# A two-block network on one core: four plain feed-forward tiles instead of three, a shorter wait at product boundaries, and the probability copies of the mixers moved to one engine

## The reference, cut to what matters

```
# first block (16 meta tokens ahead of the 1024)
h  = h + rmsnorm(z @ w_out, mix_norm_post)
u  = rmsnorm(h, ffn_norm_pre)                     # 1024 features
gt = causal_dwconv(u @ w_gate, conv_w, conv_b)    # 3 taps, 2816 features
y  = (gelu(gt) * (u @ w_up)) @ w_down
h  = h + rmsnorm(y, ffn_norm_post)
# second block, per block of 128 tokens
att: logits = q k^T/8 - slope*dist (previous and own block of keys), softmax with a sink,
     out = p @ v                                  # 8 heads of 64
mlstm: chunks, decays exp(b_t - b_s + i_s), state c_new = decay*c + (k*w)^T v
x = x + concat(rms(att), sigmoid(o)*rms(mlstm)) @ w_out
x = x + cross_attention(x, mem);  x = x + top-2 mixture of 32 experts
```

## Time and profile before

| what | value |
|---|---|
| median of 3 runs | 2849.12 us (2843.03 to 2854.50) |
| the profiled execution | 2844.58 us, its span 2842.8 us |
| PE busy in the span | 2667.1 us (94%) |
| DVE busy | 1919.3 us (68%) |
| ACT busy | 1284.8 us (45%) |
| POOL busy | 711.7 us (25%) |
| mean granted clock of TensorE | 0.974 |

### The profile page before, as it was taken

How to read it: one execution, slowest core, us unless ns; L and a number is a source line. 1 busy time by engine, 2 the same in 40 slices (tenths; PEclk the granted TensorE clock), 3 DMA queues, 4 the chain that set the end, 5 groups by cost and what they waited for, 6 DMA issues and landing times. The chain is left out here.

```text
span 2842.8 us, 38460 instructions
## 1 busy us (share of the span) xinstructions
PE 2667.1 (94%) x14346; PEld 2310.5 (81%) x14346; DVE 1919.3 (68%) x2417; ACT 1284.8 (45%) x1968; POOL 711.7 (25%) x446
## 2 busy tenths in 40 slices
PE   8989999999879999999989998889998999999993
PEld 7989999899768888878868887767785688888882
DVE  5366556363388777777884723766355899999996
ACT  4242332332343233234544204764332577777773
POOL 3000000002255555513620000005400244444441
PEclk9999999999989999999999999999998999999997
DMA  5342323343212222266742111114203799999996
GB/s 186 108 133 90 100 97 101 119 138 119 96 45 75 81 89 76 80 216 198 232 140 67 45 60 67 39 45 141 74 18 141 272 422 417 416 415 415 413 413 242
DMA packets 267201, 472.04 MB, mean 166 GB/s; under 512 B 24338, under 2 KB 183330, under 8 KB 241970
## 3 DMA queue, kind: packets, MB, share of 16 engines
q1 hardware_dynamic: 257554, 435.49, 42.8%
q0 software_dynamic: 9504, 34.61, 3.0%
HBM read 398.61 MB, written 71.43 MB: 165 GB/s over the span
## 5 line engine op out<-in xcount | busy, mean ns | idle before, releaser
L4084 DVE TENSOR_TENSOR k_w_lo<-k_raw,k_w_hi 128x2048 fp32r<-128x2048 f32 x192 | 433.4, 2287 | 34.6 <-ACT k_w_hi L4020 31.0
L4020 ACT CAST k_w_hi<-k_raw 128x2048 fp32r<-128x2048 f32 x192 | 363.2, 1912 | 64.3 <-PE bank L3938 41.3
L120 PE MATMUL bank<-u_hi,p_w_hi 128*128 128x342 f32 (+2 forms) x720 | 236.9, 329 | 8.9 <-DVEq L889 6.0
L121 PE MATMUL bank<-u_lo,p_w_hi 128*128 128x342 f32 (+2 forms) x720 | 231.1, 321 | 0.0
L122 PE MATMUL bank<-u_hi,p_w_lo 128*128 128x342 f32 (+2 forms) x720 | 230.8, 321 | 0.0
L3936 PE MATMUL bank<-k_w_hi,k_x_hi 128*128 128x512 f32 x512 | 203.0, 397 | 1.3 <-DVE k_x_lo L4090 1.0
L3938 PE MATMUL bank<-k_w_hi,k_x_lo 128*128 128x512 f32 x512 | 199.8, 390 | 0.0
L3937 PE MATMUL bank<-k_w_lo,k_x_hi 128*128 128x512 f32 x512 | 199.3, 389 | 0.0
L1467 PE MATMUL bank<-u_ffn_hi,f_w_hi 128*128 128x512 f32 (+3 forms) x520 | 170.7, 328 | 16.8 <-DVE f_inner L1757 8.4
L1468 PE MATMUL bank<-u_ffn_lo,f_w_hi 128*128 128x512 f32 (+3 forms) x520 | 167.2, 322 | 0.0
L1469 PE MATMUL bank<-u_ffn_hi,f_w_lo 128*128 128x512 f32 (+3 forms) x520 | 166.7, 321 | 0.0
(11 more groups left out here) (620 smaller groups left out, 7502.7 us busy)
## 6 DMA issues: line engine op xcount, KB each, us to landing
k_raw<-in_w_e_gate_dram SPq DMA_DIRECT2D x64, 1024.0 KB, 7.1
k_raw<-in_w_e_up_dram SPq DMA_DIRECT2D x64, 1024.0 KB, 7.7
k_raw<-in_w_e_down_dram SPq DMA_DIRECT2D x64, 1024.0 KB, 8.3
f_raw<-in_ffn_w_down_dram SPq DMA_DIRECT2D x77, 256.0 KB, 3.0
p_w<-in_w_in_dram SPq DMA_DIRECT2D x34, 512.0 KB, 4.4
f_raw<-inner_scratch SPq DMA_DIRECT2D x55, 256.0 KB, 3.5
f_raw<-in_ffn_w_gate_dram SPq DMA_DIRECT2D x22, 512.0 KB, 3.7
f_raw<-in_ffn_w_up_dram SPq DMA_DIRECT2D x22, 512.0 KB, 4.9
```

Source lines behind the costliest of these rows:

```text
L120: pe.matmul(out, wh[:, t, :], xh[t][:, c:c + n], start=t == 0, stop=False)
L121: pe.matmul(out, wh[:, t, :], xl[t][:, c:c + n], start=False, stop=False)
L4020: act.copy(wh[:, q, :], raw[:, r, :]).then_inc(hi_made, 1)
L4084: dve.tensor_tensor(wl[:, q, :], raw[:, r, :], wh[:, q, :], ALU.subtract).then_inc(lo_made, 1)
```

## The change

Three parts of the program are edited.

*Feed-forward.* Tile 3 joins `PLAIN` (`FAST_FROM = 4`), with banks of its own in `GATE` and `UP`. Tile 1 reads the same unscaled slices as tile 0; VectorE multiplies its gate by `token` in the new `keep_gate(1)` and its inner value in `multiply(1)`. So `stream_high(k)` waits until tile 1 has used slice k (`u_used` >= 8 + k + 1), and the streamed slices are first read by tile 2's gate, whose first third waits for them one by one. All `stream_low` and `sums_low` are VectorE's; GpSimd has only the low parts of weights. TensorE's wait for the first four low parts stands behind the first sum of squares, and VectorE's `low(0)` before `scale(1)`. The order of VectorE and ScalarE between tile 0 and the first tile of `seven` is new.

*Down.* TensorE no longer waits at the end of a product; ScalarE waits for `mm` or `used`, whichever belongs to the step (`multiplied`).

*Mixers.* `turn` comes in two pairs: groups 0 and 1 right after `write(i)`, groups 2 and 3 after `scores(i+1, (2, 3))` and `att_sums`. VectorE makes all four copies, two after `update(i)` and two after `logits(i+1, (2, 3))`; `keep_odd` is gone. `keys` and `h_back` use T[1], `weigh` T[0]. At the start ScalarE does `decays(0)` and `keys(0)` ahead of the exponentials, VectorE `front(0)` ahead of the second logits, and the memory's transposes are spread through iteration 0.

```diff
-PLAIN = (0, 1, 2, KF - 1)
+PLAIN = (0, 1, 2, 3, KF - 1)
+FAST_FROM = 4
@@ stage_ffn
+    GATE = {0: (0, 1, 2), 1: (5, 6, 7), 2: (2, 3, 4), 3: (0, 1, 7), KF - 1: (0, 1, 3)}
+    UP = {0: (3, 4), 1: (0, 1), 2: (5, 6), 3: (5, 6), KF - 1: (4, 5)}
@@ gpsimd
-            for q in (4, 5, 6, 7):
-                low(q)
-            for k in range(2, KD):
-                stream_low(k)
-            low(8)
-            low(9)
-            sums_low(0)
-            low(10)
-            low(11)
-            sums_low(2)
-            for q in range(12, first_operand(KF - 1) + 4):
+            for q in range(4, first_operand(KF - 1) + 4):
                 low(q)
@@ tensor
+                if n == 1 and k == 0:
+                    pe.wait_ge(g_kept, 1)            # in row_tile, before the up part
+                    if n == 2 and e == 0 and j == 1:
+                        pe.wait_ge(inner_made, 1)    # in column_tile
+                        if n == 2 and e == 0 and j == 0:
+                            pe.wait_ge(v_lo, k + 1)
-            pe.wait_ge(lo_made, 4)
             pe.wait_ge(logs, NL)
             pe.sem_inc(sq_used, 2)
...
+                if k == 0:
+                    pe.wait_ge(lo_made, 4)
                 pe.wait_ge(u_lo, k + 1)
                 row_tile(0, k)
...
+            pe.wait_ge(lo_made, 14)
+            pe.wait_ge(inner_made, 2)
+            column_tile(3, 0, LIVES, GATE[3], 0).then_inc(gmm, 1)
+            pe.wait_ge(lo_made, 16)
+            pe.wait_ge(inner_made, 3)
+            column_tile(3, 1, SEQS, UP[3], TAPS - 1).then_inc(umm, 1)
@@ scalar
-                act.wait_ge(u_used, k + 1)
+                act.wait_ge(u_used, KD + k + 1)
@@ scalar, the order after the table load
+            high(6), high(7), stream_high(0..2), gelu(0), stream_high(3), high(8), high(9), stream_high(4..7), high(10), high(11)
+            sums_high(0), gelu(1), keep_gate(2), sums_high(1), high(12), high(13), gelu(2), high(14), high(15)
+            sums_high(2), sums_high(3), keep_gate(3), high(16..19)
@@ vector, the order after the factor
+            keep_gate(0), stream(0..3), conv(0), stream(4), stream(5), stream_low(0), stream(6), stream_low(1), stream(7)
+            stream_low(2..4), multiply(0), stream_low(5..7), keep_gate(1), conv(1), sums(0), sums(1), multiply(1)
+            sums_low(0), sums_low(1), conv(2), sums(2), multiply(2), sums(3), sums_low(2), sums_low(3)
+            combine(4, 0..3), conv(3)
@@ Down, stage_down
+    def multiplied(self, engine, step):
+        i, j = divmod(step, HALF_K)
+        if j == HALF_K - 1:
+            engine.wait_ge(self.mm, 4 * (i + 1))
+        else:
+            engine.wait_ge(self.used, (HALF_K - 1) * i + j + 1)
-                else:
-                    pe.wait_ge(mm, 4 * (i + 1))
-                    pe.sem_inc(d.used, 1)
@@ stage_mixers, tensor
-                    pe.wait_ge(pt_kept_odd, 2 * c)
+                    pe.wait_ge(pt_kept, 4 * c - 1)   # keys
                 write(i)
+                turn(i, (0, 1))
                 if i < LAST:
                     scores(i + 1, (2, 3))
                 if i:
                     att_sums(i - 1)
-                turn(i)
+                else:
+                    memory_turn(0)
+                turn(i, (2, 3))
@@ stage_mixers, vector
                 update(i)
+                keep(i, (0, 1))
                 if i < LAST:
                     logits(i + 1, (2, 3))
-                keep(i)
+                keep(i, (2, 3))
@@ stage_mixers, scalar
+            decays(0)
+            keys(0)
             exponentials(0, 0)
             exponentials(0, 1)
-            decays(0)
-            keys(0)
-                keep_odd(i)
```

More of the change, by code:

```diff
@@ L1402, in std @@
         def std(n):
[L1403 removed]
+            return PLAIN.index(n) - 1
         @block.sync
@@ L1646, in _ @@
             act.preload_act_table(ACT.Gelu_apprx_tanh)
-            stream_high(0)
-            stream_high(1)
             high(6)
             high(7)
-            for k in range(2, KD):
+            for k in range(3):
                 stream_high(k)
+            gelu(0)
+            stream_high(3)
             high(8)
             high(9)
-            gelu(0)
-            sums_high(0)
-            keep_gate(1)
+            for k in range(4, KD):
+                stream_high(k)
             high(10)
             high(11)
+            sums_high(0)
+            gelu(1)
+            keep_gate(2)
             sums_high(1)
-            gelu(1)
+            high(12)
+            high(13)
+            gelu(2)
+            high(14)
+            high(15)
             sums_high(2)
             sums_high(3)
-            keep_gate(2)
-            for q in range(12, 16):
+            keep_gate(3)
+            for q in range(16, 20):
                 high(q)
@@ L1803, in fast, with keep_gate @@
                 conv(n)
+            def keep_gate(n):
+                dve.wait_ge(gmm, n + 1)
+                if n:
+                    dve.wait_ge(conv3, n)
+                for j, (c, w) in enumerate(LIVES):
+                    x = dve.tensor_tensor(g[:, c:c + w], bank[GATE[n][j]][:, 0:w], token[:, c:c + w], ALU.mult)
+                x.then_inc(g_kept, 1)
             dve.wait_ge(rstd_made, NL)
@@ L1818, in _ @@
             dve.wait_ge(h_made, KD)
-            stream(0)
-            stream_low(0)
-            dve.wait_ge(gmm, 1)
-            for j, (c, w) in enumerate(LIVES):
-                m = dve.tensor_tensor(g[:, c:c + w], bank[GATE[0][j]][:, 0:w], token[:, c:c + w], ALU.mult)
-            m.then_inc(g_kept, 1)
-            stream(1)
-            stream_low(1)
-            for k in range(2, KD):
-                stream(k)
-            dve.wait_ge(g_kept, 1)
-            conv(0)
+            keep_gate(0)
+            for k in range(4):
+                stream(k)
+            conv(0)
+            stream(4)
+            stream(5)
+            stream_low(0)
+            stream(6)
+            stream_low(1)
+            stream(7)
+            for k in range(2, 5):
+                stream_low(k)
+            multiply(0)
+            for k in range(5, KD):
+                stream_low(k)
+            keep_gate(1)
+            conv(1)
             sums(0)
-            multiply(0)
             sums(1)
-            conv(1)
+            multiply(1)
+            sums_low(0)
             sums_low(1)
+            conv(2)
             sums(2)
-            multiply(1)
+            multiply(2)
             sums(3)
+            sums_low(2)
             sums_low(3)
             for j in range(4):
-                combine(3, j)
-            conv(2)
+                combine(FAST_FROM, j)
+            conv(3)
             for n in FAST:
@@ L2716, in write, with turn @@
                 m.then_inc(umm, 1)
-            def turn(n):
-                for g in range(4):
-                    if g == 0 and n:
-                        pe.wait_ge(scaled, n)
-                    if g == 1:
+            def turn(n, groups):
+                for g in groups:
+                    if g == 0:
                         if n:
@@ L2891, in update, with keep @@
                 m.then_inc(state, 1)
-            def keep(n):
-                for g in (0, 2):
+            def keep(n, groups):
+                for g in groups:
                     dve.wait_ge(turned, 4 * n + g + 1)
@@ L2920, in _ @@
             logits(0, (0, 1))
+            front(0)
+            logits(0, (2, 3))
             maxima(0, 0)
-            logits(0, (2, 3))
-            maxima(0, 1)
-            front(0)
             queries(0)
             weights(0)
+            maxima(0, 1)
             for i in range(NB):
```

165 lines of the change are left out of this document (69 added, 96 removed).

## The result

The changed kernel takes 2828.26 us (median of 6 runs, 2825.37 to 2836.11) against 2849.84 us of the kernel before in the same session (6 runs, 2843.03 to 2855.86). The ratio is 0.9931, with a 95% interval from 0.9913 to 0.9950: faster, by 21.6 us by the medians and 19.7 us by the ratio (14.3 to 24.8). Forecast were 2828 us. The profiled execution took 2828.68 us, its span is 2826.8 us.

What follows compares the result with a forecast made beforehand. VectorE's list was taken to bound the way in, TensorE the steady tiles and nearly stage_down, a VectorE and ScalarE chain the mixers. Way in -15.0, stage_down -3.2, mixers -2.7: -20.9 from 2849.12 gives 2828 us; range 2819 to 2842.

Steps and rivals of the forecast that it cites:

- The start, -2.2: Way in: ScalarE's first square no longer waits behind four low parts of weights; 2.2 us sooner, at most 2.5.
- Tile 2's wait for the streamed slices: Way in: TensorE waits some 4.5 us in tile 2's first third for VectorE's low slices, GpSimd costing VectorE 5.9 us.
- Tile 3 as a plain tile hides VectorE's list: Way in: plain tile 3 hides its waits by a few us; tile 4 starts 15.0 us sooner.
- stage_down, -3.2: stage_down: gaps at six product boundaries go, 0.46 to 0.65 us each, 3.2 us in all; bounds 0 and 3.9.
- Mixers, +0.35 an iteration: Mixers at full clock: two copies of 0.60 us join VectorE's chain, idle of 0.75 and 0.1 goes; four iterations +1.4.
- Mixers, late iterations, -2.4: Mixers: two iterations of 20.09 us at low clock get 1.2 us shorter each, since transposes and `weigh` start sooner.
- Mixers, the start, -1.7: Mixers' start: first read 3.3 us sooner, second read 1.7 us sooner as iteration 0 is bound by ScalarE.
- Mixers, last iteration, 0: Mixers' last iteration: VectorE's copies end when they did before, so no change.
- (a): Rival, way in: VectorE keeps up, tile 2 has no wait, 7.3 us more gained, 2821 us; chance 0.13.
- (b): Rival, way in: VectorE later than counted, blocked for whole instructions or late for tile 3; gain 10 or less, 2833 to 2836; chance 0.17.
- (c): Rival, mixers: they give nothing back, 0.35 us in each of six iterations, no gain at start, +2, 2833 us; chance 0.11.
- (d): Rival, mixers: VectorE's longer chain lowers TensorE's clock, some 9 us more an iteration, six give 2882 us; chance 0.04.

Runs made afterwards that it cites:

- vector_lows: The changed kernel with the six low parts of weights q 6 to 11 on VectorE instead of GpSimd; 2825.47 us, one run.
- three_plain: The changed kernel with three plain tiles ahead of those of seven products instead of four, tile 3 being one of seven again; 2838.15 us, one run.
- last_group_scalar: The changed kernel with the copy of the fourth group of probabilities on ScalarE, the other three on VectorE; 2824.29 us, one run.
- old_start: The changed kernel with the old order at the mixers' start, exponentials ahead of decays and keys, front after both halves of the logits; 2829.82 us, one run.
- best: The changed kernel with low parts q 6 to 11 on VectorE and, from iteration 1 on, the fourth group's copy on ScalarE; 2820.16 us, 4 runs.
- both_better: The changed kernel with low parts q 6 to 11 on VectorE and the fourth group's copy on ScalarE in iteration 0 too; 2821.99 us, one run.

## Why the prediction was right, step by step

- *The start, -2.2:* right; the first square sum came 2.56 sooner, and slice 1 then waited 0.36 for VectorE's low part, the very operation named.
- *Tile 1 without a gap, -13.4:* right, no gap ahead of it nor of tile 2, and its end 13.2 us sooner after the project's sums.
- *Tile 2's wait for the streamed slices:* right in place, releaser and size: 5.2 us lost to GpSimd against 5.9, a gap of 4.16 us against some 4.5. vector_lows shows the cause: with six lows off GpSimd the loss is gone. The mechanism was wrong, and the size came near by luck. I had VectorE go on at 0.42 of its pace for the 2.02 us of each low part; the trace shows the two engines taking turns, VectorE's operation ending 1.08 to 1.09 us after GpSimd's. The 2.02 us of the earlier trace rows hold GpSimd's own wait for VectorE (alone it takes 1.29), so a low part holds one operation of VectorE up by 1.0 to 1.1 us, five times here: 5.2. My 5.9 also isn't my own count: five and a half low parts at 1.2 are 6.4 to 6.6. The Trainium skill (SBUF — State Buffer, "Who interferes with whom") has the two exclude each other for whole instructions, and the trace agrees. What did not come is the -10 that I took from it: it priced each low part at its recorded 2.02 us, with GpSimd's own waiting in it.
- *Tile 3 as a plain tile hides VectorE's list:* right; three_plain shows what it costs without it. The sum of the way in was -15.0, measured -15.1 in the first pair of traces; over all of them tile 4 stands at 123.85 to 124.87 us with this part and 139.93 to 140.45 without, a gain of 15.1 to 16.6.
- *stage_down, -3.2:* right in sum, -3.1, by two errors that cancel. A boundary is worth 0.64, not 0.53 on the mean. (The 0.46 at the lower end left out the 0.08 by which the first pass was longer; with it my terms give 0.54 to 0.65. And passes inside a product are 0.227 us apart, 29.92 / 132, not 0.233.) And "it is paced by the earlier products, so the shift passes through" failed in part: the last product is bound by VectorE, waits for `d_x` five times by 0.34 to 0.75 us, and got 0.7 us longer.
- *Mixers, +0.35 an iteration:* mis-sized, +0.12. On VectorE two copies of 0.60 came in; out went the 0.75 and 0.10 that I counted, and 0.23 that I had not, nearly all of it the wait ahead of the first copy (from the logits to it 1.52 us before, 1.32 after). The chain was the right one (last_group_scalar: -0.59 for one copy).
- *Mixers, late iterations, -2.4:* wrong. I read the clock of one execution (two iterations of 20.1 us at 0.92) as the old order's cost, and had each become 1.2 us shorter. They do not: with the new order a late one takes 20.22 to 20.27 us, with the old one it took 19.75 to 20.20. Only if the new order has fewer of them is anything left of this term, and that is open. The iteration after iteration 0, at 19.06 against 18.51, I had not foreseen either.
- *Mixers, the start, -1.7:* near in size (35.18 to 33.72, -1.5), wrong in cause as far as one trace can tell: old_start has it too.
- *Mixers, last iteration, 0:* wrong, +1.7. TensorE's timeline of after, the last read:

```profile
1884.36 0.80 PE L2691 MATMUL bank<-vm,m_s 128*128 128x129 f32 x2 [2.94 <-DVE m_s L2858]
1884.95 0.64 PE L2692 MATMUL bank<-m_c,m_qw 128*128 128x129 f32 x2
...
1887.81 3.62 PE L2716 MATMUL bank<-e_wk,e_mem 128*128 128x256 f32 x16
```

The read takes 3.45 us, 1.89 before: half clock, after a wait of 2.94 us for `weights` where before had 0.89. In last_group_scalar the wait is 2.36 and the read is at full clock; in best, after the same 2.36, the clock halves in the middle of it (passes of 0.39 us, then 0.64); the read takes 0.64 us more, and the rest of the 1.4 us that best's last iteration takes more comes behind it, at the low clock. Over all traces: after waits of 0.54 to 1.28 us (the three with the old order) the read kept the full clock; after 2.94 to 2.95 (seven) it lost it each time; after 2.36 (three) it lost it twice. So the longer wait for VectorE goes with the loss, and at 2.36 us it is one execution or another.

So of the mixers' 1.8 us in the first pair of traces, 3.2 were the two late iterations that before had and the changed kernel's first profile had not; without these it is -1.5 + 0.55 + 5 x 0.12 + 1.7 = +1.4 us, where I had -2.7. The timed runs of the part alone allow for both (3.7 gained to 2.3 lost). The total came right since the way in and stage_down carry it, and in part by luck: the mixers' terms and the price of GpSimd's work were off, and what the first pair of traces shows adds to -18.5. Of the rivals, (a) and (b) bracket the way in and neither's time came, though the blocking for whole instructions that (b) names did; (c), "the mixers give nothing back", is nearest to what the mixers do by themselves (0.6 us, 3.7 gained to 2.3 lost), but with +0.12 instead of +0.35 an iteration. (d), TensorE's clock, happens in small, and where it says, behind VectorE's longer chain, in the last iteration: +1.7 us. A late iteration costs 1.65 us, not 9, and comes with the old order as well.

## What to carry to other kernels

Measure each part of a change from a mark inside it: here an untouched stage moved by 4 us, and a stall that one execution showed in two iterations was taken for a property of the order. Where an engine that feeds TensorE is the bound, more work for TensorE (a plain tile of 22.4 us for one of 19.4) can be the cheaper way, since it covers that engine's list; and moving work off the busy engine pays only if the other engine doesn't hold it up by more than the work. Where two engines wait for each other, the recorded length of an instruction can hold the wait (2.28 us for 1.29 here): look at where instructions end, and not only at how long they are, before you put a price on them. Before giving a copy to the engine that "has time", find which engine's chain ends last in each iteration: in the steady ones it was VectorE, in iteration 0 by all signs ScalarE, and the best split differs.

## What the runs showed of the hardware that I had not expected

- A gap costs clock beyond its length, and whether it does hangs on little. Tables of stretches, kernel after behind its gap of 3.76 us, and then best behind one of 1.33:

```profile
836.56:840.56 4.00, 3.92 (x13) 3.57 (x14) 3.93 (x7) 0.00 (x0) 0.00 (x0) 0.50 0.76 226
840.56:848.56 8.00, 8.00 (x45) 7.96 (x45) 7.89 (x11) 3.29 (x6) 0.00 (x0) 0.84 0.00 0
```

```profile
828.52:832.52 4.00, 2.69 (x14) 2.12 (x15) 3.91 (x5) 0.00 (x0) 0.00 (x0) 1.00 0.33 135
832.52:836.52 4.00, 4.00 (x27) 4.00 (x27) 3.89 (x7) 0.00 (x0) 0.00 (x0) 1.00 0.67 196
```

  All seven traces with the long gap fell to 1.2 GHz (0.50) behind it. With the short gap two of three (best and both_better, tile 4 at 119.97 and 120.00) kept 2.4 GHz and one (vector_lows, 121.97) fell. Of those 2.0 us 1.4 lie behind the start of tile 2; 0.6 were there before it, where vector_lows had the lower clock at the start of tile 0 (granted clock 0.57 against 0.72 over the same 12 us).
- In the mixers the clock falls for one to three iterations at a place that changes from run to run, with the same work and the same gaps around it. What chooses the place stays open.
- VectorE and GpSimd took turns for whole instructions where both had two inputs in SBUF: in the changed kernel VectorE's operation of 1026 columns ended 1.08 to 1.09 us after the low part that it had waited for, and so lasted 2.20 to 2.33 us instead of 1.22 to 1.28. A low part of 512 columns took VectorE 0.69 us, and GpSimd 1.29 at the median and up to 2.28 with its waits.
